# A hybrid attention, pooling, memory and mixture-of-experts layer on one core: index queries turned behind the query projection, index scores behind K, pool mix behind V, and matmuls on ones in TensorE's waits

## The chip, the cores and the metric

One core of a Trainium2 chip runs the whole layer as one program. TensorE (PE) multiplies, with PEld loading its weights; VectorE (DVE), ScalarE (ACT) and GpSimd (POOL) work beside it; SyncE (SP) issues nearly all DMAs. The metric is the device time of one execution in microseconds (us); lower is better.

## The reference

The input is 256 tokens of 1024 channels, all in float32. One layer is computed:

```python
proj = rmsnorm(x) @ w_in            # -> q | k | v | index q | index k | index w | pool input | memory q
q, k, iq, ik = partial_rope(each)   # the first 16 of each head's 64 channels are rotated
sc = sum_h relu(iq_h . ik / 8) * iw_h        # index scores, 8 heads, causal
sel = top_k(sc, 64)                          # 64 keys for each query
y_attn = softmax(q . k[sel] / 8) @ v[sel]    # 8 heads of 64
y_pool = multiscale_pool(u, w_group, scale)  # causal windows of 2, 4, 8, 16, then a small mix
y_mem  = softmax(qm . km / 8) @ vm           # 4 heads, 256 memory tokens (km, vm from rmsnorm(mem))
merged = sum_i sigmoid(xn @ w_gate_i + b_i) * (y_i @ w_proj_i)
h = x + merged @ w_out
h = h + moe(rmsnorm(h))       # 32 experts, top 4, softmax gates, clamped SwiGLU
out = rmsnorm(h)
```

An expert is a 1024x2048 up-projection and a 1024x1024 down-projection. The 32 experts hold 402.7 MB of the 441.6 MB that the core reads.

## The kernel before

The program has two parts. The **front** (to about 275 us) does all up to and with the router; the **expert loop** (to 1201 us) goes through the 32 experts, 64 token slots at a time.

**Front weights.** SP loads 17 blocks of 1 to 2 MB (`FRONT`) into a ring of 4 slots; a block's load waits until the block four places before it has been split. A block is split in *units*: ACT copies a unit's high part into `unit_hi` (line 568), POOL subtracts to get `unit_lo` (line 535), and PE multiplies three times (high by high, low by high, high by low; line 1177). There are 3 unit slots, so unit u is split once PE has used unit u-3. Units 4 to 7 are IQ (index queries), 8 to 11 are Q, 12 to 15 K, 16 to 19 V, 20 and 21 QM.

**Order of the front.** Nothing schedules: each engine has its list written out by hand, and semaphores join them. PE's list is: transpose of the gains, transposes of the normed x (line 1159), projection A (index key, index weights, pool input), IQ, transposes of memory, transposes of the index queries (`iqT`, line 1207, waits until DVE has rotated them) and of the index key (`ikT`, line 1212), Q, index scores (lines 1219 and 1220), pool sums (1232), K, pool mix (1240), V, QM, the memory keys and values (1249, 1271), attention with the gates between (1306, 1290, 1315), branch projections, output projection (1364), routing, loop. ACT and DVE have lists of the same kind: ACT copies PSUM results out (606), applies the Relu of the index scores (632), and issues eight small DMAs for the expert biases (643, 644); DVE rotates (848 to 851), adds up the index scores (877, 880), takes the top 64 (894, 895), and clears halves of the key tiles (919 to 923).

**PSUM.** Results go to the 8 banks in the order of `psum_jobs`: job n takes bank n mod 8, and PE's `fill` waits until job n-8 has been emptied by its owner (ACT or DVE).

**Expert weights.** An expert is 6 pieces of 2 MB (4 up, 2 down), in 10 slots. Ten pieces are loaded ahead as the front gives its memory back; the last four of these wait for the end of the output projection and for the routing logits. From then on each load waits until PE has used the piece that had the slot (`piece_used`).

**Routing.** Output projection, router logits in two halves (`logits(0)`, `logits(1)`, line 1388), DVE's choice of four experts (`sel`), counts in `pos` and `total` (1400 to 1405), DVE's slot columns (1052), the gather of the first expert's rows (1412), ACT's copy (747), its transposes (1420), ACT's copy (751), and the first expert's up-projection (1476).

## Time and profile before

| what | value |
|---|---|
| time, median of 3 runs | 1206.98 us (1204.16 to 1207.64) |
| the profiled execution's own time | 1203.21 us |
| its span, first to last instruction | 1201.0 us |
| PE busy | 1121.9 us (93%) |
| DVE, ACT, POOL busy | 359.7, 227.3, 128.6 us |
| DMA queue q1 | 441.64 MB, 88.5% of 16 engines' span |
| DMA rate | 427 to 430 GB/s in most slices from about 330 us; 113 to 276 GB/s between 60 and 240 us |
| mean granted clock of PE | 0.987 |

The profile is one execution. "Busy" is the time with an instruction in an engine, and a wait is put down to what ended it. The granted clock is given as a share of 2.4 GHz, so 0.50 is 1.2 GHz.

### The profile page before, as it was taken

The numbers are of one execution on the slowest core, as the hardware profiler recorded it, in microseconds if no ns is written. First come the engines' busy times: TensorE is split into PE (matmuls) and PEld (weight loads), VectorE is DVE, ScalarE is ACT, GpSimd is POOL, SyncE is SP. The second block draws the span as 40 slices with busy tenths as digits, with TensorE's granted clock in tenths as the row PEclk, the third lists the DMA queues.
The fourth block names the chain that finished last, engine by engine and source line by source line (L and its number), as shares of the span: only waits on it lengthen the run. The fifth ranks groups of instructions, "written<-read, shape, count | busy, mean of one in ns | idle before, by whom it ended". The sixth has DMA issues, their size and how long they took to land.

```text
span 1201.0 us, 14123 instructions
## 1 busy us (share of the span) xinstructions
PE 1121.9 (93%) x5609; PEld 510.0 (42%) x5609; DVE 359.7 (30%) x766; ACT 227.3 (19%) x415; POOL 128.6 (11%) x59
## 2 busy tenths in 40 slices
PE   6899999999999999999999989999989899989996
PEld 5788898753333333333333323333323233333332
DVE  4593664632222222122222222222212122222222
ACT  5354454121111111111111111111111111111112
POOL 5562666400000000000000000000000000000000
PEclk9999999989999999999999999999999999999999
DMA  9554335779999999999999999999999999999993
GB/s 355 194 177 145 113 141 188 276 310 403 384 428 427 428 427 426 427 427 430 427 427 427 427 427 427 428 428 427 429 428 427 427 427 427 427 427 427 428 426 142
DMA packets 50230, 444.22 MB, mean 370 GB/s; under 512 B 6094, under 2 KB 9592, under 8 KB 25592
## 3 DMA queue, kind: packets, MB, share of 16 engines
q1 hardware_dynamic: 48256, 441.64, 88.5%
q10 hardware_dynamic: 1912, 1.66, 0.5%
q8 instruction: 50, 0.82, 0.3%
q14 instruction: 12, 0.10, 0.0%
HBM read 441.65 MB, written 1.05 MB: 369 GB/s over the span
## 4 chain that ended last, share of the span: by engine, by line
PE 61%; DMA 28%; DVE 6%; ACT 3%; issue 1%; POOL 0%; SPq 0%; DVEq 0%; ACTq 0%
PE psum L1476 23%; PE psum L1512 14%; DMA ring<-in_w_up 14%; PE psum L1177 11%; DMA gm_area<-in_w_up 10%; DMA my_area<-in_w_up 4%; PE psum L1431 3%; PE psum L1364 2%; DVE gate_area L1110 1%; DVE gate_area L1114 1%; DVE gate_area L1108 1%; PE psum L1499 1%; ACT gate_area L770 1%; PE psum L1485 1%; PE psum L1220 1%
## 5 line engine op out<-in xcount | busy, mean ns | idle before, releaser
L1476 PE MATMUL psum<-ring,gate_area 128*64 128x512 f32 x1216 | 280.0, 604 | 21.7 <-DMA ring<-in_w_up 13.4
L1080 DVE TENSOR_TENSOR h_s<-psum,h_s 128x512 f32<-128x512 f32 x132 | 82.0, 684 | 426.0 <-PE psum L1431 426.0
L1476 PEld LDWEIGHTS psum<-ring,gate_area 128*64 128x64 f32 x1216 | 85.8, 139 | 203.9 <-issue 173.3
L1512 PE MATMUL psum<-ring,gate_area 128*64 128x512 f32 x640 | 145.8, 595 | 5.3 <-ACT gate_area L770 5.3
L535 POOL TENSOR_TENSOR unit_lo<-ring,unit_hi 128x1024 fp32r<-128x1024 f32 (+1 forms) x54 | 128.2, 2380 | 95.3 <-ACT unit_hi L568 95.2
L764 ACT ACTIVATE gate_area<-gate_area 128x512 f32<-128x512 f32 x32 | 20.1, 630 | 532.0 <-DVE gate_area L1106 532.0
L1106 DVE TENSOR_SCALAR gate_area<-psum 128x512 f32<-128x512 f32 x32 | 22.1, 692 | 277.1 <-PE psum L1485 277.1
L1512 PEld LDWEIGHTS psum<-ring,gate_area 128*64 128x64 f32 x640 | 44.3, 136 | 86.3 <-issue 76.3
L1476 PE MATMUL psum<-gm_area,gate_area 128*64 128x512 f32 x256 | 60.3, 609 | 6.4 <-DMA gm_area<-in_w_up 6.4
L1431 PE MATMUL psum<-pT_s,gate_area 64*128 64x512 f32 x264 | 65.6, 615 | 0.7 <-ACT pT_s L774 0.7
L568 ACT ACTIVATE unit_hi<-ring 128x1024 fp32r<-128x1024 f32 (+1 forms) x54 | 55.5, 1032 | 47.6 <-PE psum L1177 47.4
L1412 PE MATMUL psum<-xn_area,gate_area 128*64 128x512 f32 x264 | 64.1, 606 | 0.4 <-DVE gate_area L1052 0.4
L1177 PE MATMUL psum<-xT_hi,unit_hi 128*128 128x256 f32 x208 | 62.2, 299 | 0.0
L1476 PE MATMUL psum<-qe_area,gate_area 128*64 128x512 f32 x256 | 58.8, 596 | 3.2 <-DMA qe_area<-in_w_up 3.2
L774 ACT ACTIVATE pT_s<-psum 128x512 f32<-128x512 f32 x32 | 19.1, 597 | 221.7 <-PE psum L1512 221.7
L1177 PE MATMUL psum<-xT_lo,unit_hi 128*128 128x256 f32 x208 | 58.7, 282 | 0.0
L1177 PE MATMUL psum<-xT_hi,unit_lo 128*128 128x256 f32 x208 | 58.7, 282 | 0.0
L1476 PE MATMUL psum<-my_area,gate_area 128*64 128x512 f32 x192 | 44.2, 595 | 1.2 <-DMA my_area<-in_w_up 1.2
L1431 PEld LDWEIGHTS psum<-pT_s,gate_area 64*128 64x128 f32 x264 | 22.7, 186 | 43.3 <-issue 41.7
L1177 PEld LDWEIGHTS psum<-xT_hi,unit_hi 128*128 128x128 f32 x208 | 39.7, 191 | 3.1 <-issue 2.0
L1177 PEld LDWEIGHTS psum<-xT_lo,unit_hi 128*128 128x128 f32 x208 | 39.7, 191 | 0.3
L1177 PEld LDWEIGHTS psum<-xT_hi,unit_lo 128*128 128x128 f32 x208 | 39.7, 191 | 0.0
(244 smaller groups left out, 1180.3 us busy)
## 6 DMA issues: line engine op xcount, KB each, us to landing
ring<-in_w_up SPq DMA_DIRECT2D x76, 2048.0 KB, 37.1
ring<-in_w_down SPq DMA_DIRECT2D x40, 2048.0 KB, 38.2
qe_area<-in_w_up SPq DMA_DIRECT2D x16, 2048.0 KB, 36.8
gm_area<-in_w_up SPq DMA_DIRECT2D x16, 2048.0 KB, 39.9
my_area<-in_w_up SPq DMA_DIRECT2D x12, 2048.0 KB, 35.2
xv_area<-in_w_up SPq DMA_DIRECT2D x8, 2048.0 KB, 37.9
xv_area<-in_w_down SPq DMA_DIRECT2D x8, 2048.0 KB, 38.7
my_area<-in_w_down SPq DMA_DIRECT2D x8, 2048.0 KB, 43.6
```

The lines of the kernel that those rows point to most:

```text
L535: nc.gpsimd.tensor_tensor(lo, src, hi.bitcast(F32), ALU.subtract).then_inc(lo_ready, 1)
L568: nc.scalar.activation(hi, src, ACT.Copy).then_inc(hi_ready, 1)
L764: nc.scalar.activation(sig, glu, ACT.Sigmoid, scale=ALPHA).then_inc(sig_ready, 1)
L774: nc.scalar.activation(y_s, psum[:, DOWN_BANK, :], ACT.Copy).then_inc(y_ready, 1)
L1080: nc.vector.tensor_tensor(h_s[:, b, cols], psum[:, BACK_BANKS[j], :], h_s[:, b, cols], ALU.add).then_inc(added, 1)
L1106: nc.vector.tensor_scalar(glu, psum[:, 0, :], LIMIT, None, ALU.min).then_inc(glu_ready, 1)
L1177: ins = nc.tensor.matmul(t, lhs[a], rhs[b], start=(first and n == 0), stop=(last and n == 2))
L1364: ins = nc.tensor.matmul(t, merged[:, k, b * P:(b + 1) * P], w[:, k, :], start=(k == 0), stop=(k == KC - 1))
L1412: ins = nc.tensor.matmul(psum[hf * SLOTS:(hf + 1) * SLOTS, XE_BANK, :], sel_slot[:, b, :], xn2[:, b, hf * 512:hf * 512 + 512], start=(b == ...
L1431: nc.tensor.matmul(psum[:, BACK_BANKS[j], :], putT[part, b, :], y_s[part, :], start=True, stop=True).then_inc(put_done, 1)
L1476: ins = nc.tensor.matmul(psum[lo:lo + SLOTS, c, :], lhsT, w[:, at:at + 512], start=(k == 0), stop=False)
L1512: ins = nc.tensor.matmul(psum[c * SLOTS:(c + 1) * SLOTS, DOWN_BANK, :], lhsT, w[:, at:at + 512], start=(f == 0), stop=(f == KC - 1))
```

## The change

PE, ACT and DVE lists are rewritten together with the job order:

- the projection Q moves ahead of the index query and index key transposes;
- the projection K moves ahead of the index scores; ACT splits K and copies it before the Relus, and DVE rotates K before it adds up the scores;
- V moves ahead of the pool mix;
- `keep_busy` issues matmuls of a 128x128 tile of ones by itself, into parts of PSUM banks that nothing reads then: 11 before the gains' transpose, 9 before the transposes of x, 3 before `logits(1)`, 7 before the wait for `sel`, 3 before the first gathered rows are turned and 3 before the wait that leads to the loop. The bank of `total` is claimed earlier for this.

```diff
@@ psum_jobs
     jobs += [(("memT", j), "dve") for j in range(4)]
+    jobs += [(("Q", b), "act") for b in range(B)]
     jobs += [(("iqT", j), "act") for j in range(2)] + [("ikT", "act")]
-    jobs += [(("Q", b), "act") for b in range(B)]
+    jobs += [(("K", b), "act") for b in range(B)]
     jobs += [(("idx", h), "act") for h in range(IHEADS)]
     jobs += [(("pool", j), "dve") for j in range(2)]
-    jobs += [(("K", b), "act") for b in range(B)] + [("mix", "dve")]
-    jobs += [(("V", b), "act") for b in range(B)]
+    jobs += [(("V", b), "act") for b in range(B)] + [("mix", "dve")]
@@ ScalarE
                 copy(("IQ", b), iq_s[:, b, :])
-            split(11)
+            for u in range(11, 15):
+                split(u)
+            for b in range(B):
+                copy(("Q", b), q_s[:, b, :])
...
             copy_halves("ikT", ikT[:, :], ikT_odd, lambda t: t[:, 0:S])
-            for u in range(12, 15):
+            for u in range(15, 19):
                 split(u)
             for b in range(B):
-                copy(("Q", b), q_s[:, b, :])
+                copy(("K", b), k_s[:, b, :])
             for h in range(IHEADS):
...
-            for u in range(15, 19):
-                split(u)
-            for b in range(B):
-                copy(("K", b), k_s[:, b, :])
@@ VectorE
                 rotate(q_s, b, HEADS)
+            for b in range(B):
+                dve.wait_ge(act_emptied, EMPTIED["K", b])
+                rotate(k_s, b, HEADS)
 
             for h in range(IHEADS):
...
             ins.then_inc(dve_emptied, 1)
-
-            for b in range(B):
-                dve.wait_ge(act_emptied, EMPTIED["K", b])
-                rotate(k_s, b, HEADS)
@@ TensorE
+            def keep_busy(t, count):
+
+                for _ in range(count):
+                    nc.tensor.matmul(t[:, 3 * P:4 * P], ones[:], ones[:], start=True, stop=True)
+
+            pe.wait_ge(ones_set, 1)
+            keep_busy(psum[:, 7, :], 11)
             pe.wait_ge(got_ident, 16)
...
+            keep_busy(psum[:, 7, :], 9)
             transposes("xT", xn_area, scaled, 1)
...
             transposes("memT", mem_s, scaled, 3)
 
+            project("Q", 512)
             pe.wait_ge(roped, 4)
...
-            project("Q", 512)
+            project("K", 512)
             pe.wait_ge(act_emptied, EMPTIED["ikT"])
...
-            project("K", 512)
+            project("V", 512)
             t = fill("mix")
...
-            project("V", 512)
...
             turn_h(1, 1)
+            t_total = fill("total")
+            keep_busy(t_total, 3)
             done(logits(1))
 
             t = fill("pos")
+            keep_busy(t_total, 7)
             pe.wait_ge(selected, 1)
-            pe.wait_ge(ones_set, 1)
...
-            t = fill("total")
+            t = t_total
...
             bank_free(XET_BANK)
+            keep_busy(psum[:, XET_BANK, :], 3)
             turn_gathered(0)
...
+            bank_free(PUT_BANK)
+            keep_busy(psum[:, PUT_BANK, :], 3)
             pe.wait_ge(route_done, 1)
```

On PE behind the index query projection there stood (`ident,mem_s` are memory's transposes, `ident,gate_area` the index queries', `ident,misc` the index key's, and the rows of `unit_hi` and `unit_lo` the start of Q):

```order
L1177 MATMUL psum<-unit_hi,xT_lo 128x512
L1159 MATMUL psum<-ident,mem_s 128x128 x16
L1207 MATMUL psum<-ident,gate_area 128x128 x8
L1212 MATMUL psum<-ident,misc 128x128 x2
L1177 MATMUL psum<-unit_hi,xT_hi 128x512
```

and now the 48 matmuls of Q follow memory's transposes at once; at their end stands:

```order
L1183 MATMUL psum<-unit_hi,xT_hi 128x512
L1183 MATMUL psum<-unit_lo,xT_hi 128x512
L1183 MATMUL psum<-unit_hi,xT_lo 128x512
L1214 MATMUL psum<-ident,gate_area 128x128 x8
L1219 MATMUL psum<-ident,misc 128x128 x2
L1183 MATMUL psum<-unit_hi,xT_hi 128x512
```

The ten transposes have moved behind Q's last three matmuls, and the last row is the start of K.

On DVE, before the index scores are added up (`misc` holds the index weights, `yl_area` the Relus), there stood the second half of Q's rotation:

```order
L848 TENSOR_TENSOR rope_t<-gate_area,rope 128x128
L849 TENSOR_TENSOR rope_t<-gate_area,rope 128x8x8
L850 TENSOR_TENSOR rope_t<-gate_area,rope 128x8x8
L851 TENSOR_TENSOR gate_area<-rope_t 128x8x16
L877 TENSOR_SCALAR ib_area<-yl_area,misc 128x128
L877 TENSOR_SCALAR ib_area<-yl_area,misc 128x256
```

and now, behind the whole of Q's rotation, there stands:

```order
L847 TENSOR_TENSOR rope_t<-gate_area,rope 128x128
L848 TENSOR_TENSOR rope_t<-gate_area,rope 128x8x8
L849 TENSOR_TENSOR rope_t<-gate_area,rope 128x8x8
L850 TENSOR_TENSOR gate_area<-rope_t 128x8x16
L847 TENSOR_TENSOR rope_t<-gate_area,rope 128x128
L848 TENSOR_TENSOR rope_t<-gate_area,rope 128x8x8
L849 TENSOR_TENSOR rope_t<-gate_area,rope 128x8x8
L850 TENSOR_TENSOR gate_area<-rope_t 128x8x16
L879 TENSOR_SCALAR ib_area<-yl_area,misc 128x128
L879 TENSOR_SCALAR ib_area<-yl_area,misc 128x256
```

The eight instructions of K's rotation have moved here from behind the top 64 and the pool mix.

On PE in the routing (`yl_area,memT` are the router logits, `ident,xn_area` the transposes of h, `sel` the counts, `xn_area,gate_area` the gather) there stood:

```order
L1388 MATMUL psum<-yl_area,memT 128x32 x8
L1373 MATMUL psum<-ident,xn_area 128x128 x8
L1388 MATMUL psum<-yl_area,memT 128x32 x8
L1400 MATMUL psum<-sel,before 128x32
L1401 MATMUL psum<-sel,ones 128x32
L1402 MATMUL psum<-sel,before 128x32
L1404 MATMUL psum<-sel,ones 128x32
L1405 MATMUL psum<-sel,ones 128x32
L1412 MATMUL psum<-xn_area,gate_area 64x512 x4
L1420 MATMUL psum<-ident,pT_s 128x128 x4
```

and now:

```order
L1379 MATMUL psum<-ident,xn_area 128x128 x8
L1145 MATMUL psum<-ones 128x128 x3
L1394 MATMUL psum<-yl_area,memT 128x32 x8
L1145 MATMUL psum<-ones 128x128 x7
L1408 MATMUL psum<-sel,before 128x32
L1409 MATMUL psum<-sel,ones 128x32
L1410 MATMUL psum<-sel,before 128x32
L1412 MATMUL psum<-sel,ones 128x32
L1413 MATMUL psum<-sel,ones 128x32
L1420 MATMUL psum<-xn_area,gate_area 64x512 x4
L1145 MATMUL psum<-ones 128x128 x3
L1428 MATMUL psum<-ident,pT_s 128x128 x4
```

The matmuls on ones stand ahead of each wait of this stretch; nothing else has moved in it.

## Rows read from the trace of the kernel before

**Rows 1.** Windows: us; busy of PE, PEld, DVE, ACT, POOL; granted clock; DMA share; GB/s.

```profile
252.00:256.00 4.00, 4.00 (x11) 1.85 (x10) 0.00 (x0) 0.00 (x0) 0.00 (x0) 1.00 0.00 0
257.70:278.20 20.50, 15.68 (x80) 9.69 (x79) 6.85 (x35) 6.79 (x11) 0.00 (x0) 0.75 0.96 395
278.20:318.00 39.80, 39.40 (x191) 13.76 (x192) 10.10 (x21) 3.36 (x7) 0.00 (x0) 1.00 0.97 378
318.00:1175.50 857.50, 811.20 (x3822) 279.34 (x3819) 188.90 (x389) 99.21 (x183) 0.00 (x0) 0.99 1.01 427
```

**Rows 2.** The chain that ended last, its end: start us, us, what.

```profile
1135.39 40.07 DMA gm_area<-in_w_up
```

**Rows 3.** SP's DMA queue around 257 us: start us, us, line, transfer.

```profile
257.72 0.80 SPq L468 DMA_DIRECT2D ring<-in_w_up  x2
```

**Rows 4.** PE in order of time, 33 to 54 us: start us, us, instructions, idle before.

```profile
34.23 1.91 PE L1159 MATMUL psum<-ident,mem_s 128*128 128x128 f32 x16
39.64 1.57 PE L1207 MATMUL psum<-ident,gate_area 128*128 128x128 f32 x8 [3.50 <-DVE gate_area L851]
41.29 0.78 PE L1177 MATMUL psum<-unit_hi,xT_hi 128*128 128x512 f32 x1
...
53.32 0.38 PE L1219 MATMUL psum<-ib_area,gate_area 128*128 128x128 f32 x2
53.53 0.60 PE L1220 MATMUL psum<-ib_area,gate_area 128*128 128x256 f32 x2
```

**Rows 5.** The chain that ended last, projection K: start us, us, what.

```profile
62.31 11.11 PE psum L1177 x48
```

**Rows 6.** ACT and its DMA queue, 63 to 78 us.

```profile
63.22 0.49 ACT L632 ACTIVATE yl_area<-psum 128x384 f32<-128x384 f32 x1 [0.29 <-DVE ib_area L880]
...
76.65 0.45 ACTq L644 DMA_DIRECT2D mem_s<-in_b_down  x1
77.42 1.06 ACT L568 ACTIVATE unit_hi<-ring 128x1024 fp32r<-128x1024 f32 x1 [1.93 <-PE psum L1177]
```

**Rows 7.** POOL's subtraction for unit 19.

```profile
78.56 2.40 POOL L535 TENSOR_TENSOR unit_lo<-ring,unit_hi 128x1024 fp32r<-128x1024 f32 x1 [1.56 <-ACT unit_hi L568]
```

**Rows 8.** DVE in order of time, 55 to 106 us.

```profile
55.22 1.94 DVE L848 TENSOR_TENSOR rope_t<-gate_area,rope 128x128 f32<-128x128 f32 x1 [12.38 <-ACT gate_area L606]
...
59.30 5.45 DVE L880 SCALAR_TENSOR_TENSOR ib_area<-yl_area,misc,ib_area 128x128 f32<-128x128 f32 x14
...
105.28 0.48 DVE L922 MEMSET memT<- 64x512 f32 x1 [11.16 <-PE psum L1271]
```

**Rows 9.** PE in order of time, 5 to 15 us.

```profile
5.17 0.30 PE L1148 MATMUL psum<-ident,misc 42*128 42x42 f32 x1 [5.17 <-DMA misc<-in_gains]
8.54 0.47 PE L1159 MATMUL psum<-ident,xn_area 128*128 128x128 f32 x1 [3.07 <-DVE xn_area L807]
...
14.27 0.39 PE L1177 MATMUL psum<-unit_hi,xT_hi 128*128 128x328 f32 x1 [1.60 <-DVE xT_lo L823]
```

**Rows 10.** Line 1159: duration in ns, least/median/most, and first and last start.

```profile
L1159 PE MATMUL psum<-ident,xn_area x16: 421/421/477, 8.5 to 12.2; 128*128 128x128 f32 x16
L1159 PE MATMUL psum<-ident,mem_s x16: 272/273/273, 34.2 to 35.9; 128*128 128x128 f32 x16
```

**Rows 11.** PE in order of time, the routing, and the gather in the loop.

```profile
257.52 1.87 PE L1388 MATMUL psum<-yl_area,memT 128*128 128x32 f32 x16
261.04 2.81 PE L1388 MATMUL psum<-yl_area,memT 128*128 128x32 f32 x16 [0.74 <-ACT memT L728]
265.57 0.61 PE L1400 MATMUL psum<-sel,before 128*128 128x32 f32 x2 [1.72 <-issue]
...
268.25 3.68 PE L1412 MATMUL psum<-xn_area,gate_area 128*64 128x512 f32 x8 [0.36 <-DVE gate_area L1052]
...
290.84 1.89 PE L1412 MATMUL psum<-xn_area,gate_area 128*64 128x512 f32 x8
```

**Rows 12.** Windows of the routing, columns as in rows 1.

```profile
262.00:263.00 1.00, 1.00 (x7) 1.00 (x7) 0.00 (x0) 0.28 (x1) 0.00 (x0) 0.50 1.18 508
```

## The prediction

> **What bounds the kernel now.** I read the windows first, then the end of the chain, then SP's queue. From 318 us to 1175.5 us the DMA moves 427 GB/s at a share of 1.01 while PE, busy as it is, waits for pieces [rows 1]: the expert loop is bound by the stream of weights. The chain confirms it: its last transfer takes 40.07 us from issue to landing, eight times what 2.1 MB need at 427 GB/s (4.9 us), so it stood in a queue, and it lands at 1175.46 [rows 2]. What follows, 1201.0 - 1175.5 = 25.5 us, is the last expert's compute and the output, and stays. So the end is: start of the unbroken stream + bytes / rate + holes in it + 25.5.
>
> The stream starts at 257.72 us, when the output projection has freed its weights [rows 3]; from 252 to 256 the DMA had nothing at all to do, with PE at work in every slice [rows 1]. So what the front gains ahead of 257.72 passes whole into the end. From 257.7 to 278.2 us it runs at 395 GB/s (ramp). From 278.2 to 318.0 it runs at 378 instead of 427, because loads wait for pieces that PE uses late: 39.8 x (427 - 378) / 427 = 4.6 us of holes [rows 1]. Thus a gain y in the routing, behind 257.72, passes too, but only up to 4.6 us. Past that the transfers are back to back and routing is worth nothing.
>
> **Part 1: the order.** Before, memory's transposes start at 34.23 and are issued in 16 x 0.109 (1.91 less one duration of 0.273, by 15) = 1.75 us [rows 4, 10], so PE could go on at 35.98. It waits until 39.64 for DVE's rotation of the index queries: 3.66 us. Then come ten transposes, 39.64 to 41.29, at a lowered clock, 1.65 us instead of 10 x 0.109 = 1.09: 0.56. Then Q, 41.29 to 53.32 = 12.03 us, against 11.11 for the same 48 matmuls of K [rows 4, 5]: 0.92. With Q put into the wait, the transposes come at about 35.98 + 11.11 = 47.1, 7 us after their rotation was done, and PE has no pause in which the clock falls. Sum: 3.66 + 0.56 + 0.92 = 5.1 us. The rest of the order is a permutation of the same matmuls.
>
> What hides the moves, with the index scores now 6.0 us later (start 35.98 + 11.11 + 1.09 + 11.11 = 59.3, before 53.32 [rows 4]):
> - K's rotation stands on DVE before the index sums. Q's takes from 55.22 to about 58.7, of which 1.94 us is one instruction beside POOL [rows 8]; K's copies follow K's end as Q's followed Q's end, so DVE starts to rotate at 61.2 and to add at 64.7. V takes the banks of the third and fourth Relu. The eighth Relu was at 63.22 and they come 0.78 apart, so the fourth ends at 60.6, now 66.6 [rows 6]; V starts at 59.3 + 8.9 (score and pool matmuls, 53.32 to 62.2) = 68.2. Cover 1.6 us.
> - Queued behind the last Relu on ACT are the bias DMAs and the split of unit 19. Last Relu at 63.22 + 6.0 = 69.2; eight issues of 0.45 make 3.6; split 1.06 (72.9 to 73.9); POOL 2.40: ready at 76.4 [rows 6, 7]. PE needs it three units into V, 68.2 + 3 x 2.78 = 76.5. Cover 0.1 us: this is the tightest place, cost 0 to 1, I take 0.
> - DVE's later end of the top 64 is repaid by the rotation that leaves behind it; it idled 11.16 us before line 922 [rows 8].
> - SP's loads wait on splits, which come earlier, none later. Nothing there turns.
>
> Ends for part 1: 5.1, and 3.0 if both covers fail by about a microsecond each. I take 5.1.
>
> **Part 2: matmuls on ones at the start.** No row shows one; the nearest is a 128x128 float32 matmul of line 1219, which shows as two instructions and holds PE 53.53 - 53.32 = 0.21 us at full clock [rows 4], so 0.43 at half. Eleven, from about 1.0 us (my estimate: POOL sets the ones in its first instructions), last 2.3 to 4.7 us, to 5.7 at most; the gains come at 5.17, and nothing needs their result before the first transposes of x are done. Nine more last 1.9 to 3.8 us, against a transpose at 8.54 [rows 9]: at full clock they end at 7.8, at half at 9.7, 1.1 us too late. Before, the 16 transposes of x take 421 ns each and those of memory 272 [rows 10], so the first ran at half of 2.4 GHz although the granted-clock column reads 1.00 there. At full clock the first pair of banks is ready some 0.4 us sooner (3 x 0.107 + 0.15 less duration); ACT's and POOL's chain from there to the start of A at 14.27 [rows 9] shifts by it. Ends +0.4 and -1.1; PE is busy without a break for over 4 us in the half-clock case, more than the 3.7 us of transposes after which A ran at full clock here, so I take +0.4.
>
> The Trainium skill, "TensorE: Matmul & The Clock Gate", Part 4 (PE-mode transpose), says that transposes don't count as PE being busy for the clock. By that the 16 transposes of x would not have raised it, and A would have begun at half; here A's first matmul of 328 columns lasts 0.39 us, while one of 512 columns at lowered clock lasts 0.78 [rows 4, 9]. The trace speaks against the rule for float32, the sum stays as it is; by the rule the matmuls on ones would be worth more in the routing, where eight transposes stand ahead of the fall.
>
> **Part 3: matmuls on ones in the routing.** At 262 us the granted clock is 0.50 [rows 12]. The same 16 logits instructions take 1.71 us for the first half of the tokens (257.52 to 259.23, where the transposes begin) and 2.81 for the second; the gather 3.68 against 1.89 in the loop [rows 11]. If the clock holds: 1.10 on the logits, 0.64 on the six count instructions that DVE waits for (0.21 to 0.107 each), 1.8 on the gather: 3.5 us. The added matmuls then cost nothing: three (0.64) in the 0.74 us before 261.04, seven (1.5) in the 1.72 before 265.57, three and three in ACT's two copies [rows 11]. If the clock falls all the same, seven last 3.0 us, 1.3 longer than their wait, and three 1.3 us, 0.5 longer: with both ends, y lies between -1.8 and +3.5. The only pause before the fall was those 0.74 us, and the stretch held little but 32-column matmuls; in the expert loop, with pauses of a few tenths between 512-column matmuls, the clock is 0.99 to 1.00 [rows 1]. Filling the pause with full-width work brings the stretch nearer to the loop, so I take the clock as held for most of it: y = 3.0, below 4.6, all of it passes.
>
> **Sum.** 5.1 + 0.4 + 3.0 = 8.5 us. The profiled execution took 1203.21, 2.2 more than its span; it becomes 1194.7. It lies 3.8 below the median of the runs shown, 1206.98, and I forecast the median: 1206.98 - 8.5 = **1198.5 us**.
>
> **Rivals.**
> - *The clock falls in the routing all the same.* For: the small matmuls remain, with the waits on DVE (after the counts) still empty. Against: the pause is filled. Then 5.1 + 0.4 + y of -1.5 to 0.5: about 4.8, 1202.
> - *A new wait eats half the order's gain* (unit 19, or a bank). For: a cover of 0.1 us. Against: each unit costs POOL 2.7 us and PE 2.8, so a late one is not repeated. 5.1 - 2.5 + 0.4 + 3.0 = 6.0, 1201.
> - *The front's gain does not reach the stream*, because attention between 112 and 205 us is paced by ACT and DVE in a way I read as PE's. Against: they start from the same results, all earlier. Only the routing's 3.0 is left: 1204.
> - *Slower: K's rotation holds the index sums.* Any of its eight instructions can be drawn out beside POOL as the one of 1.94 us was, which otherwise takes 0.29 or so. If POOL ran all along, 8 x 1.9 = 15 us instead of 3.5; V would wait 11.5 - 1.6 = 9.9 us for its banks, and the kernel be slower by 9.9 - 8.5 = 1.4, and by 5.1 where the clock falls too: 1208 to 1212. It decides from a rotation of 3.5 + 1.6 + 8.5 = 13.6 us. Against: POOL has only unit 18 left to do then (2.4 us), since 19 waits for V.
> - *More than forecast:* 3.5 and something from calmer waits in attention: 9.5 to 11, 1196.5.
>
> **Chances.** Forecast 50% (1196 to 1200.5), clock falls 27%, new wait 10%, not reaching the stream 6%, slower 3%, more 4%. The range from the most of the "more" case to the third rival: 1195 to 1204. Within 0.3% (3.6 us) a measurement of this kernel can hardly tell from none. Faster by over 0.3%: the forecast, seven eighths of the falling clock (its 4.8 lies close to the bound), eight tenths of the new wait, and "more": 0.50 + 0.23 + 0.08 + 0.04, less 0.02 for the scatter of the runs = 0.83. Slower 0.03, within 0.14.
>
> **What would show it.** Right: Q's first matmul directly behind memory's transposes near 35.6; the ten transposes 1.1 us long; the stream's start near 252.2; 272 ns in the first transposes; a granted clock of 1.00 in the routing, second logits 1.7 and gather 1.9 us; DMA nearer 427 in the 40 us after the first piece. Wrong: PE idle on POOL's unit 19 or on a bank at V's start; a clock of 0.50 behind the logits, with the count matmuls queued behind those on ones; an unchanged start of the stream; or a lower DMA rate in the loop, on which all of this rests.

## The result

| kernel | median of the runs, same chips | runs | profiled execution | its span | mean clock |
|---|---|---|---|---|---|
| before | 1204.16 us (1202.53 to 1207.64) | 5 | 1203.21 us | 1201.0 us | 0.987 |
| after | 1194.86 us (1194.5 to 1196.19) | 5 | 1194.78 us | 1192.5 us | 0.991 |

The ratio is 0.9919, with a 95% interval of 0.9898 to 0.9941: the change makes the kernel faster by 0.8%. The forecast was 1198.5 us, in a range from 1195.0 to 1204.0. The difference between the profiled executions was forecast as 8.5 us and is 8.43; the time forecast lies 3.6 us too high.

**Where the time came from.** The stream of the kernel after, from SP's queue (start us, us, line, transfer; the second row is the first piece that the loop gives back):

```profile
254.09 0.80 SPq L468 DMA_DIRECT2D ring<-in_w_up  x2
...
271.21 5.83 SPq L468 DMA_DIRECT2D ring<-in_w_down  x2
```

and the end of its chain, which answers to [rows 2]:

```profile
1126.94 40.08 DMA gm_area<-in_w_up
```

The stream starts at 254.09 instead of 257.72 [rows 3], 3.63 us earlier. The routing stretch from there to the first piece lasts 17.12 us instead of 20.52 (278.24 less 257.72), 3.40 less. The last transfer lands at 1167.02 instead of 1175.46, and what follows is 25.5 us as before. The 8.44 us at the last landing are thus 3.63 + 3.40, and 1.41 between the first piece and the last landing (895.81 instead of 897.22 us). The 1.41 can't be counted as the change's: a second profile of the kernel before has 895.10 there (e9 below). The agreement of 8.43 with the forecast 8.5 is to that extent luck; the two places that the change works on gave 7.0 in this pair of profiles.

The windows of the kernel after, which answer to [rows 1]:

```profile
254.09:271.20 17.11, 15.79 (x111) 11.32 (x110) 6.75 (x35) 6.79 (x11) 0.00 (x0) 1.00 0.95 384
271.20:311.20 40.00, 39.60 (x190) 13.83 (x192) 10.14 (x22) 3.59 (x7) 0.00 (x0) 1.00 1.01 420
311.20:1168.00 856.80, 811.15 (x3826) 280.55 (x3824) 188.73 (x389) 98.97 (x183) 0.00 (x0) 0.99 1.01 427
```

The routing holds a clock of 1.00 where before had a mean of 0.75, and the 40 us behind the first piece run at 420 GB/s instead of 378: the holes have shrunk from 4.6 us to 40 x (427 - 420) / 427 = 0.7. The time behind the first piece is no shorter for it, because the shorter routing has moved fewer bytes (17.11 us at 384 GB/s are 6.6 MB, 20.5 at 395 are 8.1 MB), and the 1.5 MB more that follow take about 3.6 us at 427. The long loop is the same, 427 GB/s.

**The order.** PE of the kernel after in order of time, 34 to 49 us, answers to [rows 4]:

```profile
35.00 1.91 PE L1164 MATMUL psum<-ident,mem_s 128*128 128x128 f32 x16
36.66 0.48 PE L1183 MATMUL psum<-unit_hi,xT_hi 128*128 128x512 f32 x1
...
47.65 1.04 PE L1214 MATMUL psum<-ident,gate_area 128*128 128x128 f32 x8
48.52 0.38 PE L1219 MATMUL psum<-ident,misc 128*128 128x128 f32 x2
```

Q starts behind the last transpose with no idle time in brackets, and ends 10.99 us later. The ten transposes are at full clock. But memory's transposes start at 35.00, not before 34.23 as forecast: something was lost ahead of them. And a new wait stands inside V:

```profile
77.70 0.50 PE L1183 MATMUL psum<-unit_hi,xT_hi 128*128 128x512 f32 x1 [0.63 <-POOL unit_lo L535]
```

This is unit 19, the place that the prediction called the tightest. ACT and its DMA queue in that stretch, against [rows 6]:

```profile
69.56 0.49 ACT L635 ACTIVATE yl_area<-psum 128x384 f32<-128x384 f32 x1 [0.29 <-DVE ib_area L882]
69.57 0.32 ACTq L642 DMA_DIRECT2D mem_s<-in_b_up  x1
69.93 1.31 ACTq L643 DMA_DIRECT2D mem_s<-in_b_down  x1
...
73.63 0.44 ACTq L643 DMA_DIRECT2D mem_s<-in_b_down  x1
74.12 2.01 ACT L568 ACTIVATE unit_hi<-ring 128x1024 fp32r<-128x1024 f32 x2 [2.55 <-issue]
```

The last Relu starts 0.36 us later than forecast (69.2). The second issue takes 1.31 us where its neighbours take 0.44, so the split of unit 19 begins at 74.12 instead of the 72.9 of the forecast.

**The start.** PE of the kernel after, 0 to 15 us, answers to [rows 9]:

```profile
1.00 4.17 PE L1145 MATMUL psum<-ones 128*128 128x128 f32 x22 [1.00 <-POOL ones L529]
5.75 0.22 PE L1153 MATMUL psum<-ident,misc 42*128 42x42 f32 x1 [0.58 <-DMA misc<-in_gains]
5.90 2.27 PE L1145 MATMUL psum<-ones 128*128 128x128 f32 x18
...
9.21 1.86 PE L1164 MATMUL psum<-ident,xn_area 128*128 128x128 f32 x15 [0.33 <-DVE xn_area L806]
13.87 0.39 PE L1183 MATMUL psum<-unit_hi,xT_hi 128*128 128x328 f32 x1 [2.79 <-DVE xT_lo L822]
...
14.99 0.48 PE L1183 MATMUL psum<-unit_hi,xT_lo 128*128 128x328 f32 x1
```

One matmul on ones shows as two instructions. The transposes now take 272 ns, and projection A starts at 13.87 instead of 14.27: both as forecast. But faster transposes end earlier, while ACT's, POOL's and DVE's copies still set the start of A: PE now pauses 2.79 us instead of 1.60. Half a microsecond into A the clock falls, as two windows of it show:

```profile
14.00:16.00 2.00, 2.00 (x9) 2.00 (x10) 0.56 (x2) 0.81 (x2) 1.75 (x2) 0.58 1.05 385
16.00:18.00 2.00, 2.00 (x10) 2.00 (x9) 0.00 (x0) 0.75 (x1) 1.42 (x2) 0.57 1.06 389
```

Matmuls of 328 columns take 0.48 us there instead of 0.31. What was won before A is lost in it, and more.

**The routing.** PE of the kernel after, which answers to [rows 11]:

```profile
257.41 1.97 PE L1394 MATMUL psum<-yl_area,memT 128*128 128x32 f32 x16
259.22 1.81 PE L1145 MATMUL psum<-ones 128*128 128x128 f32 x14
261.05 0.41 PE L1408 MATMUL psum<-sel,before 128*128 128x32 f32 x2
...
263.14 1.94 PE L1420 MATMUL psum<-xn_area,gate_area 128*64 128x512 f32 x8 [0.78 <-DVE gate_area L1050]
...
267.52 3.65 PE L1487 MATMUL psum<-ring,gate_area 128*64 128x512 f32 x16 [0.43 <-ACT gate_area L750]
```

The second logits take 1.97 instead of 2.81, a count's two instructions 0.41 instead of 0.61, and the gather 1.94 instead of 3.68.

### The profile page after: what moved, and what is told of

Same layout as the page of the kernel before. It is cut to its first block, busy times and chain, and to the rows that moved or that the text cites. A ratio compares the mean times of both kernels' runs of the same rounds, so it can differ in the third digit from the quotient of the medians.

```text
span 1192.5 us, 14266 instructions
## 1 busy us (share of the span) xinstructions
PE 1125.6 (94%) x5681; PEld 517.2 (43%) x5681; DVE 357.0 (30%) x766; ACT 227.2 (19%) x415; POOL 128.5 (11%) x59
## 4 chain that ended last, share of the span: by engine, by line
PE 68%; DMA 18%; DVE 7%; ACT 3%; issue 2%; POOL 0%; ACTq 0%; DVEq 0%; SPq 0%
PE psum L1487 29%; PE psum L1523 16%; PE psum L1183 11%; DMA ring<-in_w_up 11%; DMA gm_area<-in_w_up 7%; PE psum L1439 4%; PE psum L1370 2%; DVE gate_area L1106 2%; DVE gate_area L1112 2%; DVE gate_area L1108 2%; PE psum L1510 2%; ACT gate_area L769 1%; PE psum L1496 1%; PE psum L1277 1%; PE psum L1255 1%
## 6 DMA issues: line engine op xcount, KB each, us to landing
xv_area<-in_w_down SPq DMA_DIRECT2D x8, 2048.0 KB, 35.4
```

## The experiments

The theory after the result: three separate effects, each read from its own stretch (the order ahead of the stream's start, the ones at the start, the ones in the routing), and a gain at the first piece that passes whole to the end. Rivals: the clock alone does it, or the order alone, or the parts need each other, or an earlier first piece is worth nothing.

Medians, with the ratio to runs of the kernel before on the same chips:

| run | median us (range) | runs | before us | ratio (95%) | profiled us |
|---|---|---|---|---|---|
| e1_order_only | 1198.73 (1196.85 to 1199.89) | 6 | 1204.94 | 0.9950 (0.9932 to 0.9969) | 1197.27 |
| e2_ones_only | 1200.19 (1198.70 to 1201.21) | 8 | 1204.94 | 0.9962 (0.9946 to 0.9977) | 1199.40 |
| e3_order_routing | 1194.86 (1193.78 to 1196.13) | 6 | 1204.94 | 0.9920 (0.9903 to 0.9938) | 1193.78 |
| e4_order_start | 1197.46 (1196.73 to 1201.08) | 6 | 1204.94 | 0.9943 (0.9923 to 0.9963) | 1199.46 |
| e5_bias_late | 1193.70 (1192.46 to 1195.32) | 5 | 1204.45 | 0.9919 (0.9905 to 0.9932) | 1192.46 |
| e6_bridge | 1193.05 (1192.15 to 1193.89) | 4 | 1204.45 | 0.9908 (0.9893 to 0.9923) | 1193.60 |
| e7_bridge_bias | 1192.31 (1192.05 to 1193.70) | 4 | 1204.45 | 0.9908 (0.9893 to 0.9923) | 1192.05 |
| e8_transposes | 1195.73 (1193.25 to 1197.10) | 5 | 1204.45 | 0.9934 (0.9921 to 0.9948) | 1193.25 |
| e9_before_again | 1203.37 (1201.45 to 1206.48) | 12 | 1204.35 | 0.9995 (0.9983 to 1.0008) | 1203.01 |
| e10_after_again | 1194.67 (1192.69 to 1195.77) | 6 | 1204.35 | 0.9923 (0.9907 to 0.9939) | 1194.59 |
| e11_late_loop | 1197.07 (1195.83 to 1197.92) | 6 | 1204.35 | 0.9942 (0.9927 to 0.9957) | 1197.62 |
| e12_q_alone | 1202.51 (1199.56 to 1207.94) | 12 | 1204.35 | 0.9997 (0.9983 to 1.0011) | 1201.00 |

Four instants of each profile say more than its total (us, read from PE's rows of memory's transposes, SP's two rows and the chain's last landing; the last three columns are their differences):

| profile | memory's transposes | stream starts | first piece | last landing | transposes to stream | routing stretch | first piece to landing |
|---|---|---|---|---|---|---|---|
| before | 34.23 | 257.72 | 278.24 | 1175.46 | 223.49 | 20.52 | 897.22 |
| after | 35.00 | 254.09 | 271.21 | 1167.02 | 219.09 | 17.12 | 895.81 |
| e1 | 35.44 | 253.71 | 275.12 | 1169.51 | 218.27 | 21.41 | 894.39 |
| e2 | 33.84 | 257.43 | 274.59 | 1171.65 | 223.59 | 17.16 | 897.06 |
| e3 | 35.42 | 253.66 | 270.93 | 1166.03 | 218.24 | 17.27 | 895.10 |
| e4 | 34.97 | 253.91 | 276.44 | 1171.70 | 218.94 | 22.53 | 895.26 |
| e5 | 34.19 | 252.35 | 269.48 | 1164.68 | 218.16 | 17.13 | 895.20 |
| e6 | 33.76 | 252.01 | 269.14 | 1165.84 | 218.25 | 17.13 | 896.70 |
| e7 | 33.99 | 252.16 | 269.29 | 1164.31 | 218.17 | 17.13 | 895.02 |
| e8 | 35.42 | 253.68 | 271.01 | 1165.49 | 218.26 | 17.33 | 894.48 |
| e9 | 34.32 | 257.87 | 280.13 | 1175.23 | 223.55 | 22.26 | 895.10 |
| e10 | 34.71 | 253.93 | 271.06 | 1166.83 | 219.22 | 17.13 | 895.77 |
| e11 | 35.30 | 253.54 | 273.74 | 1169.78 | 218.24 | 20.20 | 896.04 |
| e12 | 34.23 | 256.91 | 278.18 | 1173.25 | 222.68 | 21.27 | 895.07 |

**e1_order_only**: the new order without any matmul on ones.

```diff
-            keep_busy(psum[:, 7, :], 11)
...
-            keep_busy(psum[:, 7, :], 9)
...
-            keep_busy(t_total, 3)
...
-            keep_busy(t_total, 7)
...
-            keep_busy(psum[:, XET_BANK, :], 3)
...
-            keep_busy(psum[:, PUT_BANK, :], 3)
```

> The new order of Q, K, V and none of the matmuls on ones. Theory (order and routing clock add up; the ones at the start lose): A begins near 14.27 and memory's transposes near 34.2 as before; Q follows near 35.9; the stream starts 5.1 less the 0.6 of unit 19, so 4.4 us sooner, at about 253.3; the clock falls in the routing as before, and the first piece is given back 20.5 us after the stream's start. Gain 4.4 us. Rival (the ones carry more than I took them for): the gain is under 3 us. Rival (routing is hidden by the stream): the gain is as large as the whole change's, 8.5 to 9.

Measured 6.2 us under before (interval 3.7 to 8.2; expected 4.4). From memory's transposes to the stream 5.22 us are won, and unit 19 causes no wait. Memory's transposes start at 35.44, not near the expected 34.2, because A began at half clock (see e3). PE in its routing:

```profile
257.12 1.94 PE L1392 MATMUL psum<-yl_area,memT 128*128 128x32 f32 x16 [0.83 <-ACT memT L727]
260.83 0.61 PE L1404 MATMUL psum<-sel,before 128*128 128x32 f32 x2 [1.76 <-DVE sel L1033]
...
263.50 3.51 PE L1416 MATMUL psum<-xn_area,gate_area 128*64 128x512 f32 x8 [0.36 <-DVE gate_area L1050]
...
269.74 5.35 PE L1481 MATMUL psum<-ring,gate_area 128*64 128x512 f32 x16 [1.32 <-ACT gate_area L750]
```

The clock falls here too, but later: the second logits still take 1.94 us, and only the counts behind the wait of 1.76 us are slow (0.61; so also in e12, while in before, e4 and e9 the second logits are slow already). The first up-projection too runs at the lowered clock, 5.35 us instead of 3.65. The order is worth its forecast by itself.

**e2_ones_only**: the old order with all the matmuls on ones.

```diff
+            pe.wait_ge(ones_set, 1)
+            keep_busy(psum[:, 7, :], 11)
...
+            keep_busy(psum[:, 7, :], 9)
...
+            t_total = fill("total")
+            keep_busy(t_total, 3)
...
+            keep_busy(t_total, 7)
             pe.wait_ge(selected, 1)
-            pe.wait_ge(ones_set, 1)
...
-            t = fill("total")
+            t = t_total
...
+            keep_busy(psum[:, XET_BANK, :], 3)
...
+            bank_free(PUT_BANK)
+            keep_busy(psum[:, PUT_BANK, :], 3)
```

> The old order, with all the matmuls on ones. Theory: start of A 0.4 us sooner, but the pause of 2.8 us behind the faster transposes can let the clock fall, which gives back up to 1.2; the index transposes' wait and its fallen clock stay. Routing 3.4 us shorter, all of it passed on by the stream. Gain 2.6 to 3.8 us, and a stream that starts -0.4 to +0.8 us from 257.7. Rival (routing is hidden by the stream): gain under 1.

Measured 4.7 us under before (interval 2.8 to 6.5; expected 2.6 to 3.8). The stretch to the stream is 223.59 us as in before, the routing 17.16. So neither part needs the other. A's clock did not fall in this profile, though PE paused as in the kernel after, and memory's transposes come at 33.84, 0.39 earlier: this is the forecast start term, in an execution in which nothing takes it back.

**e3_order_routing**: the kernel after without the 11 and 9 at the start.

```diff
-            keep_busy(psum[:, 7, :], 11)
...
-            keep_busy(psum[:, 7, :], 9)
```

> The whole change without the 20 matmuls on ones at the start. Theory: nothing falls in A, so memory's transposes start at 34.2 instead of 35.0; stream at about 253.3; routing held at full clock, 17.1 us from the stream's start to the first piece given back. Gain 7.8 to 8.6, that is 0.8 us better than the whole change where the whole change's clock falls in A. Rival (the ones at the start are worth their 0.4 us, and the fall in A was one execution's chance): 0.4 us worse than the whole change.

Measured 1194.86, the median of the kernel after itself, 10.1 us under before (interval 7.5 to 11.7). At this precision the ones at the start are worth nothing. The expected start of memory's transposes at 34.2 did not come: it is 35.42. Its A shows why, and why the ones did not lose either:

```profile
14.41 0.61 PE L1181 MATMUL psum<-unit_hi,xT_hi 128*128 128x328 f32 x1 [1.61 <-DVE xT_lo L822]
14.82 0.47 PE L1181 MATMUL psum<-unit_lo,xT_hi 128*128 128x328 f32 x1
```

Without them A began at half clock here, though in the kernel before it began at full (0.39, then 0.31 us). Of the eight profiles without ones at the start, four (before, e5, e9, e12) have A at full clock; in three (e1, e3, e11) it begins at half, and in e8 it begins at full and falls 1.1 us later. Memory's transposes then start at 34.2 to 34.3, and at 35.3 to 35.4.

**e4_order_start**: the kernel after without the ones in the routing.

```diff
-            keep_busy(t_total, 3)
...
-            keep_busy(t_total, 7)
...
-            keep_busy(psum[:, XET_BANK, :], 3)
...
-            keep_busy(psum[:, PUT_BANK, :], 3)
```

> The whole change without the 16 matmuls on ones in the routing. Theory: stream's start as in the whole change (about 254.1), then 20.5 us to the first piece given back, with the clock at 0.50 behind the first router logits. Gain 3.6 us. Rival (order alone keeps the clock in the routing up, since the phase of the stretch has moved): 17 to 18 us and a gain of 7.

Measured 2.6 us above e3, in the profiles 5.7. Against before that is a gain of 7.5 us in the medians (4.5 to 9.3 by the interval), where 3.6 was expected, and 3.75 in the profiles; why the medians gain more stays open. The rival with the same gain of 7 is out, since it wanted a stretch of 17 to 18 us: the routing stretch is 22.53 us, with a clock of 0.68 from 255 to 262 us. PE waits 0.44 us for unit 19.

**e5_bias_late**: e3 with ACT's eight bias DMAs moved behind the splits 19 to 22 and V's copies.

```diff
+            for u in range(19, 23):
+                split(u)
+            for b in range(B):
+                copy(("V", b), v_s[:, b, :])
             act.wait_ge(bank_filled, FILLED["memT", 3])
             for q in range(4):
...
-            for u in range(19, 23):
-                split(u)
-            for b in range(B):
-                copy(("V", b), v_s[:, b, :])
             split(23)
```

> E3 (new order, matmuls on ones in the routing alone) with ACT's eight bias DMAs moved behind the splits of units 19 to 22 and the copies of V. Theory: unit 19 is late because its split is queued behind these issues; without them it is split when PE has used unit 16, and PE's pause before V's fourth unit (0.6 us) goes. Stream 0.7 us sooner, gain on E3 0.7 us. Rival (POOL's pace, 2.7 us a unit, makes the pause): nothing changes.

The profile is 1.3 us better than e3's, but not where the edit is (0.7 was expected there): from memory's transposes to the stream it takes 218.16 us against 218.24. The 1.2 us are A at full clock (34.19 against 35.42), which is chance here, since the two kernels are the same up to that point. E3 had no wait on unit 19 to remove; so this pair doesn't decide the edit's worth.

**e6_bridge**: the kernel after with twelve more matmuls on ones, behind the transposes of x, to bridge the pause ahead of A.

```diff
             transposes("xT", xn_area, scaled, 1)
+            keep_busy(psum[:, 7, :], 12)
```

> The whole change and 12 more matmuls on ones between the transposes of x and the projection A, where PE paused 2.8 us. Theory: the pause lets the clock fall in A in some executions; filled, A runs at full clock from 13.9 on, memory's transposes start at 33.8 in every profile, and the kernel gains 0.4 to 1.2 us on the whole change. Rival (they hold A up): A starts later than 14.0 and the kernel loses.

```profile
10.86 2.84 PE L1145 MATMUL psum<-ones 128*128 128x128 f32 x24
13.84 0.39 PE L1184 MATMUL psum<-unit_hi,xT_hi 128*128 128x328 f32 x1
...
14.21 0.31 PE L1184 MATMUL psum<-unit_hi,xT_lo 128*128 128x328 f32 x1
```

The pause is gone, A starts as early as in the kernel after and stays at 0.31 us, and memory's transposes start at 33.76 instead of 35.00. With the pause left, the clock fell in A in three of four profiles (after, e4, e10; not in e2); with it filled, in neither of two (e6, e7). So the pause very likely let it fall, on six profiles. The median is 1.8 us under the kernel after, in another set of runs; the intervals of the two ratios to before overlap (0.9893 to 0.9923 here, 0.9898 to 0.9941 there). In ACT's queue the second bias DMA is issued in its usual time, and there is no wait on unit 19:

```profile
68.69 0.43 ACTq L643 DMA_DIRECT2D mem_s<-in_b_down  x1
...
72.00 2.20 ACT L568 ACTIVATE unit_hi<-ring 128x1024 fp32r<-128x1024 f32 x2 [1.67 <-issue]
```

**e7_bridge_bias**: e6 with the bias DMAs late as in e5.

```diff
+            for u in range(19, 23):
+                split(u)
+            for b in range(B):
+                copy(("V", b), v_s[:, b, :])
             act.wait_ge(bank_filled, FILLED["memT", 3])
             for q in range(4):
...
-            for u in range(19, 23):
-                split(u)
-            for b in range(B):
-                copy(("V", b), v_s[:, b, :])
             split(23)
...
             transposes("xT", xn_area, scaled, 1)
+            keep_busy(psum[:, 7, :], 12)
```

> Both at once: the whole change, the 12 matmuls of E6 and the late bias DMAs of E5. Theory: the two gains lie in series ahead of the stream's start and add: stream at about 252.2, gain on the whole change 1.1 to 1.9 us. Rival (the first piece is awaited from the stream, as PE did for 0.58 us in E3): the start of the stream moves, the end by the same, since that wait moves with it.

This is the lowest median, 1192.31 us, but the late DMAs add nothing to e6 that can be told (the ratios are equal). E6 had no wait on unit 19 either, so neither e5 nor e7 tests the late DMAs against that wait. Four runs of it and four of e6 all lie between 1192.05 and 1193.9; the eleven runs of the kernel after (with e10) between 1192.69 and 1196.19.

**e8_transposes**: e3 with each matmul on ones in the routing replaced by two transposes of ones.

```diff
-                    nc.tensor.matmul(t[:, 3 * P:4 * P], ones[:], ones[:], start=True, stop=True)
+                    nc.tensor.transpose(t[:, 3 * P:4 * P], ones[:], ident[:])
+                    nc.tensor.transpose(t[:, 3 * P:4 * P], ones[:], ident[:])
```

> E3 with each matmul on ones in the routing replaced by two transposes of ones by the identity, which hold PE as long (0.21 us a pair at full clock). The Trainium skill's page TensorE: Matmul & The Clock Gate says in Part 4 that transposes don't count as busy for the clock: by that it falls behind the first logits, seven pairs take 3.0 us, the first piece comes back 21 to 23 us after the stream's start, and the gain on E3 is -3 to -5. Theory from the traces (16 transposes alone preceded a rise): the clock holds, 17.2 us, same time as E3.

```profile
256.09 0.27 PE L1145 MATMUL psum<-ident,ones 128*128 128x128 f32 x1
...
256.99 1.97 PE L1393 MATMUL psum<-yl_area,memT 128*128 128x32 f32 x16
...
262.72 1.94 PE L1419 MATMUL psum<-xn_area,gate_area 128*64 128x512 f32 x8 [0.78 <-DVE gate_area L1050]
```

The clock holds just as well: 17.33 us against 17.27, with the same logits and gather. The median is 0.9 us above e3's, with overlapping intervals. The Trainium skill, "TensorE: Matmul & The Clock Gate", Part 4 (PE-mode transpose), says that the full clock does not engage for transposes, since they don't count as PE being busy in the same way. If they did nothing for the clock, this stretch would have been like those without filler, 20.5 to 22.5 us. In this float32 stretch they kept the clock up as matmuls on ones do, in the one profile taken.

**e9_before_again** and **e10_after_again**: the kernel before and the kernel after, both unchanged.

> The kernel before once more, for a second profile. Theory (the clock's fall in the routing costs a different amount from execution to execution, and the profile of before was one of its cheaper cases): the stretch from the stream's start to the first piece given back is not 20.5 us again but 20.5 to 22.5, memory's transposes start at 34.2 or 35.4, and the runs scatter over 4 us or more, about 1204.5. Rival (the scatter lies in the DMA's rate in the loop): that stretch is 20.5 again and what differs is the time from the first piece given back to the last landing, 897.2 us in the profile of before.

> The changed kernel once more. Theory: routing 17.1 to 17.3 us again, since nothing falls there; memory's transposes at 33.8 or 35.0; V's fourth unit waits only if one of ACT's bias DMA issues is drawn out as in its first profile (1.31 us instead of 0.44). Runs scatter under 3 us, about 1194.9. Rival as for the kernel before: the scatter is as wide.

The first measures how much one profile of before may say. Its routing:

```profile
268.53 3.68 PE L1412 MATMUL psum<-xn_area,gate_area 128*64 128x512 f32 x8 [0.36 <-DVE gate_area L1052]
...
274.74 5.35 PE L1476 MATMUL psum<-ring,gate_area 128*64 128x512 f32 x16 [1.13 <-ACT gate_area L751]
```

The stretch takes 22.26 us, as the first up-projection is slow too. The routing without ones was 20.52, 21.41, 22.53, 22.26 and 21.27 us in five profiles, a mean of 21.6. The profile that the prediction rests on was the mildest; with ones (and nothing added behind them) it was 17.12 to 17.33 in eight. E10 repeats the kernel after: A at half clock, here from its first matmul on (34.71), and a wait for unit 19 (0.76 us) behind a drawn-out second DMA issue (1.43 us). Its six runs spread over 3.1 us, the twelve of e9 over 5.0.

**e11_late_loop**: e3 with 19 instead of 3 matmuls on ones in the last wait, so that the loop starts late at an unchanged clock.

```diff
-            keep_busy(psum[:, PUT_BANK, :], 3)
+            keep_busy(psum[:, PUT_BANK, :], 19)
```

> E3 with 16 more matmuls on ones (3.4 us) directly before PE's entry into the loop. Theory: the end follows the first piece given back, whatever made it late: that piece 3.0 to 3.4 us later than in E3, about 20.4 us after the stream's start, DMA at 380 instead of 420 GB/s in the 40 us behind it, 3 us slower than E3. Rival (the stream is its own limit, since PE waited for a transfer in E3): 0 to 0.5 us slower.

The first piece comes 2.81 us later than in e3 (3.4 less the 0.58 that PE waited there, see below), the last landing 3.75 later, the median 2.2. E3's and e11's windows of the same 40 us, and the 40 us behind e11's own first piece:

```profile
270.93:310.93 40.00, 39.60 (x190) 13.81 (x192) 10.16 (x22) 3.60 (x7) 0.00 (x0) 1.00 1.01 420
```

```profile
270.90:310.90 40.00, 39.60 (x190) 13.57 (x188) 9.40 (x20) 3.18 (x6) 0.00 (x0) 1.00 0.95 381
...
274.00:314.00 40.00, 39.60 (x192) 13.72 (x190) 10.42 (x22) 3.81 (x7) 0.00 (x0) 1.00 0.95 382
```

420 falls to 381 or 382 GB/s, near to what before had. The delay becomes holes in the stream and passes to the end, as the prediction has it for y. That the rest of a further gain would be lost was not tried, but it is near: in e3 PE waits for the prefetch for the first time:

```profile
267.24 3.65 PE L1485 MATMUL psum<-ring,gate_area 128*64 128x512 f32 x16 [0.58 <-DMA ring<-in_w_up]
```

**e12_q_alone**: only Q moved, and on ACT with it the splits of units 12 to 14 and Q's copies; the projections K and V, the splits from 15 on, K's copies and K's rotation stay where before has them; no ones.

```diff
@@ ScalarE
-            split(11)
+            for u in range(11, 15):
+                split(u)
+            for b in range(B):
+                copy(("Q", b), q_s[:, b, :])
...
-            for u in range(12, 15):
-                split(u)
-            for b in range(B):
-                copy(("Q", b), q_s[:, b, :])
@@ TensorE
             transposes("memT", mem_s, scaled, 3)
 
+            project("Q", 512)
             pe.wait_ge(roped, 4)
...
-            project("Q", 512)
```

> Of the new order only Q ahead of the index transposes; K, V, their splits, copies and rotation stand where they stood before, and no matmuls on ones. Theory: 5.2 us are won as in E1, but between the index transposes and the index scores PE now waits for ACT, which copies Q and the transposes first (1.1 + 1.0 + 0.75 us behind the split of unit 14): 2.5 to 3 us of pause at about 48.5. 2.5 to 3 us slower than E1. Rival (moving Q alone does it, K and V are moved for nothing): as fast as E1.

```profile
46.91 1.03 PE L1212 MATMUL psum<-ident,gate_area 128*128 128x128 f32 x8
47.78 0.38 PE L1217 MATMUL psum<-ident,misc 128*128 128x128 f32 x2
50.80 0.79 PE L1223 MATMUL psum<-ib_area,gate_area 128*128 128x128 f32 x2 [2.63 <-ACT pT_s L615]
```

and ACT's copies, two of Q and then two of the index queries:

```profile
48.07 2.04 ACT L606 ACTIVATE gate_area<-psum 128x512 f32<-128x512 f32 x4
```

The transposes' results must be copied by ACT before the scores can use them. In before Q covered that copy. With Q ahead, the wait has only changed its place: 2.63 us of pause, and the clock is 0.50 in the scores behind it (52 to 54 us). The median, 1202.51 us, can't be told from before's, and is 3.8 above e1's. Only 0.8 us are won from transposes to stream, against 5.2 in e1. So of the two orders tried, only the one with K ahead of the scores makes Q's move pay. About 1.0 us of the pause is Q's own copies, which stand on ACT ahead of the transposes' copies; an order of ACT with these last was not tried.

## Why the prediction was right, and where it failed

**What bounds the kernel** held. The table has nearly one length from the first piece to the last landing, 894.4 to 897.2 us, for every front, and e11 shows by experiment that a later first piece makes a later end. That length moves by up to 2.8 us (0.3%), and by 2.1 us between two profiles of the same kernel before (897.22 and 895.10); what moves it was not found. Before's first profile was the longest, which is 1.4 of the 8.44 us.

**Part 1, 5.1 us** held: 5.2 in all seven profiles of the new order without a wait on unit 19 (223.5 less 218.16 to 218.27). K's rotation took from 61.65 to 65.04, 3.4 us (forecast 61.2 to 64.7), with one drawn-out instruction beside POOL:

```profile
61.65 1.86 DVE L847 TENSOR_TENSOR rope_t<-gate_area,rope 128x128 f32<-128x128 f32 x1 [8.58 <-ACT gate_area L606]
...
64.14 0.29 DVE L847 TENSOR_TENSOR rope_t<-gate_area,rope 128x128 f32<-128x128 f32 x1
```

The slower rival needed all eight like the first and got one; V didn't wait for a bank. *Unit 19*, taken at 0 with bounds of 0 and 1, cost 0.7 to 1.0 us in the three profiles that show the pause (219.09, 218.94 and 219.22 against 218.2). These are the three in which one of the DMA issues ahead of the split took 1.11 to 1.43 us instead of 0.44; in the five others of the new order with these issues at that place (e1, e3, e6, e8, e11) none did, and there was no wait. So the place was named rightly, and its value of zero left no room for one slow issue.

**Part 2, +0.4 us** failed in its working. The 0.40 us at the start of A are there, but the step "PE is busy without a break for over 4 us ..., so I take +0.4" looked at what raises the clock and not at the pause that the faster transposes themselves lengthen, from 1.60 to 2.79 us. In the kernel after the clock falls in A, and memory's transposes come 0.77 later, not 0.4 earlier. E6 and e7, which fill the pause, start them at 33.76 and 33.99, which is 0.47 and 0.24 sooner where 0.4 was forecast; two profiles make that cause very likely, not certain. The loss does not show in medians (e3 against after), which fits A running partly at half clock in four of the eight profiles without ones too.

**Part 3, y = 3.0 us** was the right mechanism and too small: 3.40 against before's profile and 21.6 - 17.1 = 4.5 against the mean of five. I kept 0.5 back for a clock that was held only "for most of it"; it was held all along, in every profile with ones. And the one profile did not show that the fall often takes the first up-projection with it. In runs the size is less certain than in profiles: the medians give 2.6 (e4 less e3), 3.9 (e1 less e3) and 4.7 (before less e2). Nor is it known which of the four groups of matmuls on ones holds the clock: without them it fell in the second logits in three profiles and only at the wait for `sel` in two (e1, e12), and no run left single groups out. The rival of 27%, that the clock falls all the same, did not occur once in nine profiles.

**The step that put the time outside my range** is the last one of the sum: "It lies 3.8 below the median of the runs shown, 1206.98, and I forecast the median". 1203.21 less 8.5 is 1194.7; the profiled execution after took 1194.78 and the median is 1194.86. The 1206.98 was the middle of three runs which lay between 1204.16 and 1207.64; in the four sets since then the kernel before has medians from 1204.16 to 1204.94 (23 runs in the largest: 1204.35, from 1201.17 to 1208.05). In the set with the kernel after it is 1204.16, which accounts for 2.8 of the 3.6 us. The other 0.8 is that the medians differ by 9.3 us there (9.7 with e10, 10.1 with e3), not 8.5. The profiles explain it in part: by the means of the two profiles of each kernel the first piece comes 8.05 us sooner (279.19 and 271.14), with the routing worth more than forecast and unit 19 and the start less; the last 1.2 us or so of the medians' difference are in none of the instants read, and stay open. The range began at 1195.0, 0.3 above my own 1194.7: it left out the plain alternative of counting from the profiled execution. By its own rule, 11 us off 1206.98, it would even have begun at 1196.0.

## What to carry to other kernels

Where a kernel is bound by a stream behind its front, read two instants, the stream's start and its first returned piece, and price each edit by the one it moves; totals of a few runs scatter more than such edits are worth. Filler matmuls must cover the pause that the faster work ahead of them opens, not only the pause seen before. When a wait is filled with other work, ask what that work used to cover: here Q had hidden ACT's copy, and K in its place kept the gain.

## What the runs showed of the hardware

- The granted clock fell behind pauses of 2.79 us (kernel after, A), 1.82 us (e8, A) and 2.63 us (e12), and in the routing, in a stretch of 32-column matmuls with waits of 0.74 to 1.76 us. With the routing's waits filled it did not fall there in any of nine profiles, nor in A in the two with A's pause filled; with A's pause of 2.8 us left it stayed up in one of four (e2).
- Whether a held clock narrows the scatter is open: before spreads over 6.9 us in 23 runs on one chip and 3.1 in 9 on another; on that other chip e6 and e7 spread over 1.8 in 8 runs, but e8, whose routing held its clock too, over 3.9 in 5.
- The clock column reads 1.00 at the start of an execution while the matmuls run at half: 0.47 us for 328 columns in e3 from 14.8 to 17.3 us, with windows of 1.00. Durations are the safer reading there.
- The second DMA issue on ACT's queue took 1.31 us instead of 0.44 in the kernel after (1.11 and 1.43 in e4 and e10, 0.43 in e6). One of the eight issues was also drawn out in e2 (the seventh, 1.20 us) and in e5 (1.02 us, without ones at the start), none in the other nine profiles; why stays open.
